# y halves, odd-head order, a three-pass first slab, and five attention-stage weight remainders on GpSimd

## The chip, the cores and the metric

The kernel runs on one core of one Trainium2 chip. TensorE multiplies matrices, VectorE, ScalarE and GpSimd do elementwise work, and SyncE and GpSimd issue DMAs. The time is that of the device, in microseconds, for one execution of the whole program on 256 tokens of width 1024; lower is better. Engine times below come from one profiled execution.

## What is computed

Two blocks run one after the other. The first has a retention layer and a sparse-attention layer, each with a mixture of experts. The second has three branches on one input projection:

```python
def second_block(x, w_in, ...):
    u = h @ w_in
    z, xbc, dt_f_raw, dt_b_raw, q, k, v, gate_logits = jnp.split(u, ...)
    y_ssd = ssd_branch(z, xbc, dt_f_raw, dt_b_raw, ...) @ w_proj_ssd
    y_att = attention_branch(q, k, v) @ w_proj_attn
    mix = (gates[:, :, 0] * y_ssd + gates[:, :, 1] * y_att) @ w_out
    h = layer_norm_2(alpha * h + mix, ln1_g, ln1_b)
    f = jnp.square(jax.nn.relu(h @ w_up)) @ w_down
    return layer_norm_2(alpha * h + f, ln2_g, ln2_b)
```

`ssd_branch` starts with a centred depthwise convolution of five taps over the 24 x 128 channels of `xbc`, then scans in both directions, multiplies by silu(z) and normalizes by group. `attention_branch` has 12 heads with windows of three dilations.

## The kernel before

Every engine has its own program, written out by hand; the engines meet at semaphores (`wait_ge` on one, `then_inc` on the other). The program goes through the stages in the list `STAGES`.

**Weight slabs.** Dense weights come in slabs of 128 x 4096 floats through three slots of `ring`, loaded by SyncE (`dense`). A matrix product is made from three products of rounded parts: `high(q)` on ScalarE (L1639) rounds a half slab into `w_rounded`, `low(q)` on VectorE (L2105) writes the remainder, `ring` minus `w_rounded`, into `ring_low`, and TensorE (`split_columns`, L854) multiplies rounded by rounded, rounded by remainder and remainder by rounded, interleaved. A half slab is 48 matmuls of 256 columns. The counters `w_high` and `w_low` count halves in order; `q` numbers the halves over the whole program, and `HQ["att"]` is the first half of the attention stage. `w_rounded` has two buffers, so `high(q)` waits until TensorE is done with half q - 2.

**Start.** SyncE loads the transposed tokens and the two halves of the first slab, then the next two slabs. GpSimd waits for the first slab and then issues the retention constants (`cret`), the constants of all stages (`call`), the tokens (`h`) and the first gain and bias, in this order, and folds the router's weights. VectorE makes the activations' remainder, `low(0)`, `low(1)`, and then waits for `cret` before `low(2)`. TensorE starts with `pe.wait_ge(x_low, 1)` and `split_slabs("ret_in", 8, r_hT)`, whose first half waits for `low(0)`.

**Attention stage.** Its 12 halves of weights (`xbc_half(n)`, six slabs) feed the convolution; they are laid between the steps of the 12 heads. For a head `hd` TensorE does `att_transposes` (L970), for even heads also `att_scores` of the next pair (L1404), then `att_products` (L1425) and `xbc_half(hd + 2)`. ScalarE copies the transposes out of PSUM (L1933), runs `high(HQ["att"] + hd + 3)`, copies a finished slab to `c_raw` (L1941), makes the exponentials for head `hd + 2` (L1922) and the silu after the convolution (L1914). VectorE does, for each head, `att_largest(hd + 2)` (L2706, L2710, L2711: mask, row maximum, its scaling), `att_out(hd)` (L2716: products out of PSUM), `low(HQ["att"] + hd + 3)`, and `conv(hd)` (L2692 the first tap of two channels, L2694 the other four). Four PSUM banks go round for transposes, scores and products; `take_aux(b)` waits until bank b - 4 is read, so an even head's products wait for `att_out` of the odd head before. GpSimd copies `s_a3` at the start of the stage (L790) and has nothing else until the scan.

**Scan stage (ssd).** Sixteen steps p, four to a group g. VectorE makes clamped decays (`clamp`, L2823), `weigh_decay` (L2812), `take_y` (L2833: y out of PSUM, half a group at a time), `root_diagonal` (L2858) and remainders; ScalarE the exponentials (L1982); GpSimd the scaled inputs (L808). TensorE's `diagonals(p)` (L1528) write y of group g into one pair of PSUM banks, the same pair for every group. A group's first `diagonals` waits in `take_pair` until the whole pair has been read for the group before.

**Work on GpSimd that is read below.** `plain_features` (L766) adds two 128 x 2048 tensors; `fold_norm` has small products (L745, L749).

Of the kernel before, what the change touches and what calls it, by code (L numbers as in the profile page):

```python
# [22 lines left out]
F32 = mybir.dt.float32  # L23
# [129 lines left out]
def build(nc, x_tok, x_feat, slabs, experts_w, c_all, c_ret, c_nsa, c_ssd, c_att, w_pattn, ln_gb, out):  # L153
    ctx = ExitStack()
    with ctx:
# [286 lines left out]
        decay_ready = sem("decay_ready")  # L442
        rows_ready, ssd_exp_ready = sem("rows_ready"), sem("ssd_exp_ready")
        ssd_y_ready, square_ready = sem("ssd_y_ready"), sem("square_ready")
        root_ready, root_diag_ready, y_low = sem("root_ready"), sem("root_diag_ready"), sem("y_low")
        mix_ready, f_ready = sem("mix_ready"), sem("f_ready")
        x_high, x_low, x_plain = sem("x_high"), sem("x_low"), sem("x_plain")
# [274 lines left out]
        def _(pool):  # L722

            pool.wait_ge(slab_loaded[0], 16)
            pool.dma_start(cret, c_ret).then_inc(stage_loaded, 16)
            pool.dma_start(call[:], c_all).then_inc(call_loaded, 16)
            pool.dma_start(h[:], x_tok).then_inc(h_loaded, 16)

# [60 lines left out]
            for u in range(3):  # L789
                nc.gpsimd.tensor_copy(s_a3.rearrange("p (r i u h) -> p r i u h", r=2, i=NT, u=3)[:, :, :, u, :],  # L790
                                      s_a.rearrange("p i (r h) -> p r i h", r=2)).then_inc(copies_ready, 1)
            nc.gpsimd.memset(s_half, -0.5).then_inc(pool_chain, 1)

            def root(g):
# [26 lines left out]
        def _(pe):  # L821
# [68 lines left out]
            def first_slab(stage, src, ln, signal, count):  # L890

                dst = take_pair(PJ[stage])
                for half in range(2):
# [23 lines left out]
                                                            stop=(half == 1 and n == 2 and k == 3))  # L917
                    last.then_inc((half_done, slab_done)[half], 1)

            def split_slabs(stage, n, src, first=0):  # L920
                for s in range(first, n):
                    dst = take_pair(PJ[stage] + s)
                    for q in (HQ[stage] + 2 * s, HQ[stage] + 2 * s + 1):
                        (split_columns if by_columns(q) else split_rows)(dst, q, src)
# [70 lines left out]


            SPLIT = ((0, 0), (0, 1), (1, 0))
            pe.wait_ge(x_low, 1)
            split_slabs("ret_in", 8, r_hT)

            def ret_transposes(hd):

# [432 lines left out]
            for hd in range(ATT_H - 2):  # L1435
                att_transposes(hd)
                if hd % 2 == 0:
                    att_scores(hd // 2 + 1)
                att_products(hd)
                xbc_half(hd + 2)  # L1440
            for hd in (ATT_H - 2, ATT_H - 1):
                att_transposes(hd)
            for hd in (ATT_H - 2, ATT_H - 1):
# [75 lines left out]
            def diagonals(p):  # L1519

                g, c = divmod(p, 4)
                j = PJ["ssd"] + 2 * g
                dst = (take_pair(j) if c == 0 else pair(j))[:, c * T:(c + 1) * T]
                pe.wait_ge(xdt_ready, p + 1)
                pe.wait_ge(m_ready, 2 * p + 2)
                for n, (r, i, a, b, at) in enumerate(((0, 0, 0, T, 0), (0, 1, P, T, 256), (1, 0, 0, P, 384), (1, 1, 0, T, 512))):
                    for e in range(2):
                        last = nc.tensor.matmul(dst[e * DH:(e + 1) * DH, a:b], s_xdt[:, p % 4, r, i, e * DH:(e + 1) * DH],  # L1528
                                                s_M[:, (2 * p + e) % 4, at:at + b - a], start=(n == 0), stop=(n == 3))
                last.then_inc(diag_done, 1)  # L1530
# [559 lines left out]
        def _(dve):  # L2090
# [630 lines left out]
            low(HQ["att"] + 2)  # L2721
            for hd in range(ATT_H - 2):
                att_largest(hd + 2)
                att_out(hd)
                low(HQ["att"] + hd + 3)
                conv(hd)
            att_out(ATT_H - 2)
            att_out(ATT_H - 1)
            for hd in (ATT_H - 2, ATT_H - 1):
# [97 lines left out]
            def take_y(g, half):  # L2827
# [7 lines left out]
                if half:  # L2835
                    last.then_inc(pair_out[j % 2], 1)
                    wait_pair_out(dve, j)
                else:
                    link(last)

            def gate_y(g):

# [300 lines left out]
```

## Time and profile before

| what | us |
|---|---|
| median of 3 runs (1504.03 to 1506.44) | 1504.74 |
| the profiled execution | 1504.41 |
| its span, first to last instruction | 1502.6 |
| TensorE busy (matmul), share of the span | 1425.3, 95% |
| VectorE busy | 800.4, 53% |
| ScalarE busy | 551.8, 37% |
| GpSimd busy | 58.0, 4% |

The shares are means over stages with different limits: in the expert stages the DMA queues are full, in the dense stages TensorE is. The attention stage lies between about 955 and 1053 us of the span, the scan stage between about 1095 and 1207. Busy times of an engine count overlapping instructions once.

### The profile page before, as it was taken

The page shows a single profiled execution, that of the slowest core. Times are in us where ns is not written, and L with a number is a line of the kernel's source. Part 1 is how long each engine was busy: PE and PEld are TensorE (multiplying, and loading weights), DVE is VectorE, ACT ScalarE, POOL GpSimd, SP SyncE. Part 2 cuts the span into 40 slices and gives each one's busy share as a digit, 9 for nine tenths or more (in the row PEclk, how much of TensorE's full clock was granted, in tenths as well). Part 3 has the DMA queues.
Part 4 walks back from the last instruction along what each step waited for, and adds up shares of the span by engine and source line. Part 5 has one row for each costly group of instructions (what it writes and reads, how often), then busy time and mean ns, then how long its engine had stood idle before and what let it go on. Part 6 is the DMA issues. An engine that isn't in the chain of part 4 may idle for free. (4 is left out here: it accounts for less than half of the span.)

```text
span 1502.6 us, 20186 instructions
## 1 busy us (share of the span) xinstructions
PE 1425.3 (95%) x8684; PEld 1064.0 (71%) x8684; DVE 800.4 (53%) x1105; ACT 551.8 (37%) x701; POOL 58.0 (4%) x79
## 2 busy tenths in 40 slices
PE   6999999999988999999999979999988899999997
PEld 6987785443437788874434349899967799799886
DVE  4645552221227657551222254699899955655545
ACT  3344442111013354421101024588656553344432
POOL 1000000000003000000000010100111100000000
PEclk9999999999999999999999999999998999999999
DMA  8553686999994540389999974533411144445451
GB/s 342 176 215 114 252 334 265 429 427 427 429 426 165 175 162 1 113 314 416 427 427 428 428 331 165 210 113 123 159 57 57 57 168 169 177 154 202 170 194 58
DMA packets 27745, 355.16 MB, mean 236 GB/s; under 512 B 2881, under 2 KB 4929, under 8 KB 5761
## 3 DMA queue, kind: packets, MB, share of 16 engines
q1 hardware_dynamic: 25840, 341.85, 57.4%
q0 software_dynamic: 1808, 11.93, 2.1%
q8 instruction: 72, 1.18, 0.3%
q14 instruction: 25, 0.20, 0.0%
HBM read 352.72 MB, written 1.05 MB: 235 GB/s over the span
## 5 line engine op out<-in xcount | busy, mean ns | idle before, releaser
L2105 DVE TENSOR_TENSOR ring_low<-ring,w_rounded 128x2048 fp32r<-128x2048 f32 (+1 forms) x124 | 290.5, 2347 | 244.2 <-ACT w_rounded L1639 236.1
L1639 ACT ACTIVATE w_rounded<-ring 128x2048 fp32r<-128x2048 f32 (+1 forms) x124 | 235.2, 1899 | 311.7 <-PE ps L854 97.4
L854 PE MATMUL ps<-split,w_rounded 128*128 128x256 f32 x960 | 228.9, 286 | 17.5 <-DVE ring_low L2105 16.5
L854 PE MATMUL ps<-split,ring_low 128*128 128x256 f32 x736 | 209.7, 285 | 0.0
L854 PEld LDWEIGHTS ps<-split,w_rounded 128*128 128x128 f32 x960 | 168.7, 193 | 18.7 <-issue 16.2
L854 PE MATMUL ps<-hT_low,w_rounded 128*128 128x256 f32 x512 | 145.3, 284 | 0.0
L854 PEld LDWEIGHTS ps<-split,ring_low 128*128 128x128 f32 x736 | 141.2, 192 | 0.0
L884 PE MATMUL ps<-w_rounded,split 128*128 128x512 f32 (+1 forms) x352 | 124.5, 394 | 2.9 <-DVE split L2926 1.5
L2398 DVE TENSOR_SCALAR split<-ps,work 128x1024 fp32r<-128x1024 f32 x14 | 18.0, 1284 | 198.2 <-PE ps L1154 198.2
L1122 PE MATMUL ps<-work 128*64 128x512 f32 x448 | 100.9, 597 | 4.5 <-DMA work<-experts_w 4.5
L884 PE MATMUL ps<-ring_low,split 128*128 128x512 f32 (+1 forms) x256 | 99.0, 387 | 0.0
L854 PEld LDWEIGHTS ps<-hT_low,w_rounded 128*128 128x128 f32 x512 | 98.9, 193 | 0.0
L1122 PE MATMUL ps<-ring,work 128*64 128x512 f32 x416 | 93.9, 596 | 0.0
L960 PE MATMUL ps<-w_rounded,split 128*128 128x512 f32 x320 | 87.1, 392 | 0.0
L884 PEld LDWEIGHTS ps<-w_rounded,split 128*128 128x128 f32 x352 | 66.8, 190 | 17.8 <-DVE split L2926 1.9
L1122 PEld LDWEIGHTS ps<-work 128*64 128x64 f32 x448 | 30.8, 137 | 63.6 <-issue 59.5
L1729 ACT ACTIVATE work<-ps 128x512 f32<-128x512 f32 x32 | 17.4, 594 | 149.2 <-PE ps L1102 149.2
L1154 PE MATMUL ps<-work 128*64 128x512 f32 x320 | 70.8, 593 | 0.1
L960 PEld LDWEIGHTS ps<-w_rounded,split 128*128 128x128 f32 x320 | 59.9, 188 | 13.5 <-issue 0.8
L1122 PEld LDWEIGHTS ps<-ring,work 128*64 128x64 f32 x416 | 28.3, 137 | 52.9 <-issue 52.9
L2393 DVE TENSOR_TENSOR work<-work,ps 128x512 f32<-128x512 f32 x16 | 11.0, 688 | 98.4 <-PE ps L1122 98.4
L884 PE MATMUL ps<-w_rounded,hT_low 128*128 128x512 f32 (+1 forms) x160 | 60.7, 380 | 0.0
(368 smaller groups left out, 2438.3 us busy)
## 6 DMA issues: line engine op xcount, KB each, us to landing
ring<-slabs SPq DMA_DIRECT2D x65, 2048.0 KB, 8.1
work<-experts_w SPq DMA_DIRECT2D x48, 2048.0 KB, 20.7
ring<-experts_w SPq DMA_DIRECT2D x36, 2048.0 KB, 16.9
w_plain<-experts_w SPq DMA_DIRECT2D x12, 2048.0 KB, 16.7
gb<-ln_gb POOLq DMA_DIRECT2D x6, 1024.0 KB, 8.8
ring<-slabs SPq DMA_DIRECT2D x2, 1024.0 KB, 8.7
hT<-x_feat SPq DMA_DIRECT2D x1, 1024.0 KB, 5.0
work<-c_ret POOLq DMA_DIRECT2D x1, 1024.0 KB, 11.9
```

The costliest lines, as they stand in the source:

```text
L854: last = nc.tensor.matmul(dst[:, at:at + T], w3[a][:, k, c * P:(c + 1) * P], src[b][:, k, :], start=(k == 0 and t == 0), stop=(k == KC - 1 ...
L884: last = nc.tensor.matmul(dst[:, i * 512:i * 512 + cols], src[a][:, 4 * half + k, i * P:(i + 1) * P], w3[b][:, k, :], start=(half == k == ...
L960: last = nc.tensor.matmul(dst[i][:, c * 512:(c + 1) * 512], src(a, s)[:, 2 * half + k, i * P:(i + 1) * P], w3[b][:, k, c * 512:(c + 1) * 512],
L1122: last = nc.tensor.matmul(bank(b)[e * CAP:(e + 1) * CAP, :], m_xT[:, e2 % 3, 4 * half + k, e * CAP:(e + 1) * CAP], w4[:, e, k, :], start=( ...
L1154: last = nc.tensor.matmul(bank(4 + c)[e * CAP:(e + 1) * CAP, :], m_heT[:, 2 * half + k, e * CAP:(e + 1) * CAP], w4[:, e, k, c * 512:(c + 1 ...
L1639: nc.scalar.activation(rounded_half(q), half_of(ring, q), ACT.Copy).then_inc(w_high, 1)
L1729: last = nc.scalar.activation(m_xT[:, (2 * t + e) % 3, 4 * half:4 * half + 4, :], tok[:, :, e, :], ACT.Copy)
L2105: V.tensor_tensor(half_of(ring_low, q), half_of(ring, q), rounded_half(q).bitcast(F32), ALU.subtract).then_inc(w_low, 1)
L2393: V.tensor_tensor(m_he, m_sg, bank(1), ALU.mult).then_inc(ps_.he_ready, 1)
L2398: V.tensor_scalar(m_yh, bank(4, 2), m_w[:, e2:e2 + 1], None, ALU.mult).then_inc(ps_.weighed, 1)
```

## The change

Five things change, all in the hand-written orders.

- GpSimd waits for the third slab before it issues `c_all`, the tokens and what follows.
- TensorE's first half slab is done by a new function in three passes (rounded by rounded, rounded weights by remainder of the activations, remainder of the weights), each with its own wait.
- In the attention stage TensorE does `xbc_half(hd + 2)` before `att_products(hd)` for odd heads; VectorE does `att_out(hd)` after `conv(hd)` for odd heads.
- The remainders `low(HQ["att"] + hd + 3)` of even heads 0, 2, 4, 6 and 8 are made by GpSimd; VectorE's next remainder waits for them.
- The first two `diagonals` of a group wait for the first half of `take_y` of the group before, and the third waits for the second half.

```diff
@@ block.gpsimd
             pool.dma_start(cret, c_ret).then_inc(stage_loaded, 16)
+            pool.wait_ge(slab_loaded[2], 16)
             pool.dma_start(call[:], c_all).then_inc(call_loaded, 16)
             pool.dma_start(h[:], x_tok).then_inc(h_loaded, 16)
...
+            for hd in range(0, ATT_H - 2, 2):
+                q = HQ["att"] + hd + 3
+                pool.wait_ge(w_high, q + 1)
+                pool.wait_ge(w_low, q)
+                nc.gpsimd.tensor_tensor(half_of(ring_low, q), half_of(ring, q), rounded_half(q).bitcast(F32),
+                                        ALU.subtract).then_inc(w_low, 1)
             nc.gpsimd.memset(s_half, -0.5).then_inc(pool_chain, 1)
@@ block.tensor
+            def start_half(dst):
+
+                pe.wait_ge(x_high, 1)
+                pe.wait_ge(w_high, 1)
+                w3 = split_weights(0, KC)
+                for n in range(3):
+                    if n == 1:
+                        pe.wait_ge(x_low, 1)
+                    elif n == 2:
+                        pe.wait_ge(w_low, 1)
+                    for c in range(2):
+                        for k in range(KC):
+                            last = nc.tensor.matmul(dst[:, c * T:(c + 1) * T], w3[n // 2][:, k, c * P:(c + 1) * P],
+                                                    r_hT[n % 2][:, k, :], start=(n == c == k == 0),
+                                                    stop=(n == 2 and c == 1 and k == KC - 1))
+                last.then_inc(half_done, 1)
...
-            pe.wait_ge(x_low, 1)
-            split_slabs("ret_in", 8, r_hT)
+            first_pair = take_pair(PJ["ret_in"])
+            start_half(first_pair)
+            split_columns(first_pair, 1, r_hT)
+            split_slabs("ret_in", 8, r_hT, 1)
...
-                att_products(hd)
-                xbc_half(hd + 2)
+                if hd % 2:
+                    xbc_half(hd + 2)
+                    att_products(hd)
+                else:
+                    att_products(hd)
+                    xbc_half(hd + 2)
...
-                dst = (take_pair(j) if c == 0 else pair(j))[:, c * T:(c + 1) * T]
+                dst = (take_pair(j) if p == 0 else pair(j))[:, c * T:(c + 1) * T]
+                if c == 0 and g:
+                    pe.wait_ge(y_half_out, g)
+                if c == 2 and g:
+                    wait_pair_out(pe, j - 2)
@@ block.vector
                 att_largest(hd + 2)
-                att_out(hd)
-                low(HQ["att"] + hd + 3)
+                if hd % 2 == 0:
+                    att_out(hd)
+                if hd % 2:
+                    dve.wait_ge(w_low, HQ["att"] + hd + 3)
+                    low(HQ["att"] + hd + 3)
                 conv(hd)
+                if hd % 2:
+                    att_out(hd)
...
-                    link(last)
+                    last.then_inc(y_half_out, 1)
+                    dve.wait_ge(y_half_out, g + 1)
```

## Rows read from the trace of the kernel before

**Rows 1.** Busy time by engine: stretch, length, busy (instructions), granted clock, DMA.

```profile
967.00:1049.10 82.10, 78.20 (x643) 74.44 (x642) 77.87 (x147) 69.39 (x100) 0.00 (x0) 1.00 0.36 129
1095.00:1207.00 112.00, 95.49 (x754) 81.16 (x754) 105.84 (x206) 63.05 (x68) 16.14 (x27) 0.91 0.18 64
```

**Rows 2.** TensorE's waits, 966 to 1049: us in total, times, longest.

```profile
PE ps L1425 <- ACT work L1933: 3.9, 5, 0.8
```

**Rows 3.** TensorE's longest wait in the scan, 1095 to 1207.

```profile
PE ps L1528 <- DVE work L2833: 10.3, 3, 4.8
```

**Rows 4.** VectorE's waits, 1095 to 1210.

```profile
DVE ring_low L2105 <- ACT w_rounded L1639: 3.4, 4, 0.9
DVE work L2833 <- PE ps L1528: 1.7, 1, 1.7
```

**Rows 5.** In order of time, an odd head to the next: start, length, instruction.

```profile
991.75 0.60 PE L970 MATMUL ps<-call,work 128*128 128x128 f32 x4
992.88 1.90 ACT L1639 ACTIVATE w_rounded<-ring 128x2048 fp32r<-128x2048 f32 x1
994.93 2.28 DVE L2105 TENSOR_TENSOR ring_low<-ring,w_rounded 128x2048 fp32r<-128x2048 f32 x1
997.13 0.61 DVE L2692 TENSOR_SCALAR work<-work 128x256 f32<-128x256 f32 x2
997.77 3.63 DVE L2694 SCALAR_TENSOR_TENSOR work<-work 128x256 f32<-128x256 f32 x8
...
1000.97 1.90 ACT L1639 ACTIVATE w_rounded<-ring 128x2048 fp32r<-128x2048 f32 x1
1001.43 1.10 PE L1425 MATMUL ps<-work 128*128 128x64 f32 x8
1002.34 0.36 PE L854 MATMUL ps<-split,w_rounded 128*128 128x256 f32 x1
...
1008.18 0.60 PE L970 MATMUL ps<-call,work 128*128 128x128 f32 x4
```

**Rows 6.** VectorE by line, two heads (983.3 to 999.8): busy, mean ns of one.

```profile
L2710 DVE TENSOR_REDUCE work<-work 128x2 f32<-128x512 f32 x2 | 1.4, 686 | 0.1
L2706 DVE SCALAR_TENSOR_TENSOR work<-work,ps 128x512 f32<-128x512 f32 x2 | 1.4, 684 | 0.1
L2716 DVE COPY work<-ps 128x128 f32<-128x128 f32 x2 | 0.6, 285 | 0.0
```

**Rows 7.** In order of time: GpSimd beside VectorE's remainders, and GpSimd's fold.

```profile
24.78 1.73 POOL L745 TENSOR_TENSOR folded<-call 128x128 f32<-128x128 f32 x1 [10.50 <-DMA call<-c_all]
27.62 0.40 POOL L749 TENSOR_TENSOR folded<-call 128x128 f32<-128x128 f32 x1
...
465.18 2.28 DVE L2105 TENSOR_TENSOR ring_low<-ring,w_rounded 128x2048 fp32r<-128x2048 f32 x1
465.44 6.51 POOL L766 TENSOR_TENSOR hT<-split,split 128x2048 f32<-128x2048 f32 x1 [2.90 <-DVE split L2113]
467.38 6.72 DVE L2105 TENSOR_TENSOR ring_low<-ring,w_rounded 128x2048 fp32r<-128x2048 f32 x1
```

**Rows 8.** In order of time: scalings by a column, beside GpSimd and without.

```profile
1137.93 3.48 POOL L808 TENSOR_TENSOR work<-work 128x256 f32<-128x256 f32 x6
1140.51 0.98 DVE L2858 TENSOR_SCALAR work<-call,work 128x128 f32<-128x128 f32 x2
...
1202.26 0.48 DVE L2858 TENSOR_SCALAR work<-call,work 128x128 f32<-128x128 f32 x2
```

**Rows 9.** In order of time: the start of the program.

```profile
10.73 2.29 DVE L2105 TENSOR_TENSOR ring_low<-ring,w_rounded 128x2048 fp32r<-128x2048 f32 x1 [0.70 <-ACT w_rounded L1639]
13.17 0.55 PE L854 MATMUL ps<-split,w_rounded 128*128 128x256 f32 x1 [13.17 <-DVE ring_low L2105]
23.95 2.29 DVE L2105 TENSOR_TENSOR ring_low<-ring,w_rounded 128x2048 fp32r<-128x2048 f32 x1 [7.95 <-DMA work<-c_ret]
27.42 0.28 PE L854 MATMUL ps<-split,w_rounded 128*128 128x256 f32 x1
```

More of the change, by code:

```diff
@@ L444, in build @@
         ssd_y_ready, square_ready = sem("ssd_y_ready"), sem("square_ready")
+        y_half_out = sem("y_half_out")
         root_ready, root_diag_ready, y_low = sem("root_ready"), sem("root_diag_ready"), sem("y_low")
```

## The prediction, made before the change was run

> **What bounds the kernel now.** I read the three places that the change touches, each by the same views in the same order: the busy time of the engines in the stretch, then who waits there and for whom, then the instructions in order of time. In the attention stage (heads 0 to 9) TensorE is busy 78.20 of 82.10 us and VectorE 77.87 [rows 1]: two engines are full at once, and a microsecond taken from one is worth only what the other lets through. TensorE's only waits there are five of 0.78, for ScalarE's copy of an odd head's transposes [rows 2]; they come to 3.9 us. In the scan stage of the second block (1095 to 1207) VectorE is busy 105.84 of 112.00 us and TensorE 95.49 [rows 1]. The reader sees TensorE wait 10.3 us in three waits for the VectorE line that takes y out of PSUM [rows 3], while VectorE itself waits for ScalarE four times 0.85 and for TensorE once, 1.7, at the end [rows 4]. VectorE sets that stage. At the start, TensorE begins at 13.17, after the first weight remainder, and later has its second slab at 27.42 [rows 9].
>
> **Three-pass first slab and the held-back loads: about -1.0 us.** The first half needs only the rounded weights to begin. Its remainder starts on VectorE at 10.73, which is when rounding is done; the old first matmul came 0.15 after the remainder's end at 13.02 [rows 9], so the new one comes at about 10.85, 2.3 earlier. Of its 48 matmuls the first 16 want no remainder and the next 16 only that of the activations, which VectorE has just finished; a slab's 96 now take 27.42 - 13.17, 0.15 each, so the 33rd comes 4.7 after the first, past 13.02. The second slab doesn't profit as much: its remainder stands on VectorE behind the wait for the retention constants and starts at 23.95 [rows 9]. That load is issued as before, ahead of the new wait, so I leave its landing where it is. The remainder ends at 26.24, TensorE goes on at 26.39, against 27.42: 1.03 gained, and a wait of 1.3 opens in front of it. The bounds are 0 and 2.3 (were the constants to land early enough). The constants for later and the token tile move behind the third slab on GpSimd's queue, with the first gain and bias load and the router's fold queued behind them; the first reader on TensorE is the second retention head's transposes, nine slabs on, which is what hides them: cost nothing; without that cover they would cost what they land later.
>
> **The y halves: 0.** The wait of the first two diagonals of a group moves from the second half's copy to the first half's, made two steps earlier; the 10.3 us of TensorE waits [rows 3] go. But the next thing on the path is VectorE's own queue, which runs on without a pause through these three places: all its waits in the stage are the four on ScalarE, whose rounding is behind exponentials that wait for VectorE, and the 1.7 us at the last diagonals [rows 4], which the change leaves alone. TensorE comes early to the next wait for VectorE. Bounds: a gain of up to 3.4, if the ScalarE waits all went, and a loss of 0.3; I take 0, the row of the saturated engine being the nearer.
>
> **The odd-head order alone: no gain.** TensorE now does the odd head's half slab before its products, so the 0.78 is covered. In return VectorE copies the odd products out after the convolution, and the next even head's products wait for that bank. Follow the rows from an odd head's transposes [rows 5]: transposes at 991.75, rounding ends at 994.78, remainder starts at 994.93 (3.18 in all), convolution follows 2.20 later and takes 4.27 (997.13 to 1001.40), the copy 0.28 [rows 6], the even products 0.91 (1001.43 to 1002.34), the half slab 5.84 (to 1008.18), and there the next odd transposes stand: 16.68 us around. The pair of heads takes 16.43 now (991.75 to 1008.18). So with the remainders left on VectorE or moved at no cost, the pair stays at 16.4 to 16.7; the 3.9 of rows 2 turn into waits for a PSUM bank.
>
> **Five remainders on GpSimd: about +11 us.** Off VectorE go five times 2.20 (one remainder, start to next start [rows 5]). On GpSimd the nearest row is an addition of the same size, 128x2048 with two inputs in SBUF: 6.51 [rows 7]. It is shorter than it looks. It began at 465.44, while VectorE's remainder ran until 467.46; the next remainder, which takes 2.28 everywhere else, took 6.72 and ended at 474.10, which is 2.15 after GpSimd's end at 471.95 [rows 7]. The two took turns: GpSimd's own part is 471.95 - 467.46, 4.49. A small GpSimd multiplication shows the same: 1.73 begun under a remainder, 0.40 alone [rows 7]. So a remainder on GpSimd holds off whatever on VectorE can't run beside it for 4.49.
>
> What can't? Remainders, by these rows. The convolution's first tap is a scaling of one SBUF tensor by a column; the nearest row is the two scalings of the identity, 0.98 for two beside a running GpSimd, 0.48 with GpSimd idle [rows 8]: held too. The other eight instructions of a convolution take two SBUF inputs, as the remainders do, but none ran beside GpSimd in this trace. The Trainium skill (SBUF — State Buffer, section "Who interferes with whom") has it that an instruction of VectorE with two SBUF inputs contends with a GpSimd instruction that reads SBUF, and that whoever is first keeps the pair for its whole length. By that rule all ten are held and the sum is the one below; by the rows alone the eight are open, which is the first rival. The stage's free work is what reads PSUM or reduces: 0.69 + 0.69 a head [rows 6].
>
> The sum for a pair: 16.43 - 2.20 + 4.49 = 18.72 if the whole hold falls on held work, 17.3 if one head's 1.38 lies under it. That is +0.9 to +2.3 a pair. Where the hold falls into the loop of the odd head (its convolution, then the copy, then the even products), the pair takes 16.68 + 4.49 = 21.2, +4.7. GpSimd gets its rounded half at about 1002.87 in the time of this trace and TensorE wants the remainder at 1008.8, 0.6 after the transposes at 1008.18 [rows 5]: 4.49 and up to 0.48 for the instruction in progress fit, so TensorE doesn't wait for GpSimd but for VectorE. Of five transfers I take the first at nothing (VectorE has just been waiting for the slabs there and has room), one at 4.7, three at 2.3, and with the order's small gain for the first pair, -0.5, that is 11.1; say +11. Bounds: 5 x 0.9 = 4.5 with nothing in the loop, and 4.7 + 4 x 2.3 = 13.9. VectorE's wait for the previous remainder, new on odd heads, has its own remainder, the convolution and the copy queued behind it, and the even products wait for that copy; it is over before the rounding that the same remainder needs, so it costs nothing. After the heads VectorE's own list (combination weights, gates) sets when TensorE goes on, so the delay is passed on.
>
> **Sum.** The profiled execution is 1504.41 (span 1502.6), within 0.4 of the median 1504.74. 1504.4 - 1.0 + 0 + 0 + 11 = 1514.4.
>
> **The rivals.** First, on the other side: the eight two-input instructions of the convolution are not held. Then GpSimd's 4.49 lies beside them, the pair stays at the odd loop's 16.4 to 16.7, and the whole is 1504.4 - 1.0 + 0.2 = 1503.6: not slower. It decides where the convolution's row beside a running GpSimd stays at 0.48 an instruction. For it speaks that no row here shows that case; against it, that the remainders and the scalings are both held. Chance 0.12. Second: TensorE's waits do come back, 10.3 in the scan and 3.9 at the heads, on top of free transfers: 1504.4 - 1.0 - 14.2 = 1489; it needs VectorE to have slack that rows 1 and 4 don't show; half of it, 1497, is as far as I can imagine. Chance 0.06. Third: GpSimd's subtraction needs 6.5 of its own. Then a pair takes 16.43 - 2.20 + 6.5 = 20.7, five of them +21.5, the whole 1525; against it, the turns in rows 7. Chance 0.04. That the moved remainders don't run beside anything (GpSimd busy with older work) can be left out: its queue is empty between the copies at the start of the stage and the scan.
>
> **How the numbers follow.** The forecast, held convolutions, has 0.78: 1514.4, from 1506.6 (4.5, and 2.3 at the start) to 1518.3 (13.9 and a start gain of 0). The range 1506.0 to 1519.0 holds that case and leaves out the first rival and most of the others. What a measurement of this kernel can tell from no change is about 0.2%, 3 us. Slower by more: 0.74 of the forecast and 0.04 of the third rival, 0.78. Within: the rest of the forecast and most of the first rival, 0.15. Faster: the second and a part of the first, 0.07.
>
> **What would show it.** Right: GpSimd rows of 4.5 to 4.9 in the attention stage; in each pair a scaling or a tap of the convolution (or the small scaling of the row maxima) stretched by 3 to 4.5; TensorE's 0.78 gone and waits on VectorE's copy of odd products in their place, 1 to 7 us each; the scan stage as long as now with its 10.3 moved to other VectorE lines; the second slab near 26.4. Wrong: taps that stay at 0.48 beside GpSimd, a pair of heads at 15.7 (the order paid), or a scan stage under 110 us.

## The result, and the profile after

The changed kernel takes 1515.99 us (median of 4 runs, 1515.22 to 1522.02) against 1505.59 of the kernel before beside it: 10.4 more, a ratio of 1.0070 (95% interval 1.0053 to 1.0088). The profiled execution took 1516.13, its span is 1514.3, 11.7 more than before. Line numbers move with the change: L854 became L862, L970 L995, L1425 L1452, L1528 L1563, L2105 L2140, L2692 and L2694 L2727 and L2729, L2706 to L2711 L2741 to L2746, L2716 L2751, L2833 L2873.

The span splits at two marks, the transposes of head 0 and those of head 10, read from the timelines:

| stretch | before | after | difference |
|---|---|---|---|
| to the transposes of head 0 | 966.99 | 969.29 | +2.30 |
| heads 0 to 9 | 82.11 | 91.54 | +9.43 |
| from there to the end | 453.50 | 453.47 | -0.03 |

Busy times of the stretches after, as in [rows 1]: the five pairs of heads, all ten heads, and a piece of the scan stage as long as the one before.

```profile
969.29:984.65 15.36, 15.36 (x131) 14.82 (x129) 13.38 (x18) 8.47 (x14) 4.61 (x1) 1.00 0.38 138
984.65:1009.57 24.92, 17.41 (x131) 16.79 (x130) 20.05 (x35) 15.73 (x23) 4.65 (x1) 0.86 0.23 85
1009.57:1026.15 16.58, 15.41 (x131) 14.80 (x130) 16.19 (x28) 13.96 (x21) 4.59 (x1) 1.00 0.36 127
1026.15:1043.59 17.44, 15.41 (x130) 14.79 (x130) 17.02 (x30) 14.82 (x22) 4.59 (x1) 1.00 0.34 121
1043.59:1060.83 17.24, 15.42 (x131) 14.80 (x130) 16.82 (x30) 14.57 (x22) 4.64 (x2) 1.00 0.33 123
969.29:1060.83 91.54, 79.00 (x643) 76.00 (x641) 83.46 (x137) 67.55 (x98) 23.07 (x6) 0.96 0.32 116
1107.26:1219.26 112.00, 96.61 (x758) 82.03 (x759) 106.12 (x207) 64.16 (x68) 18.45 (x27) 0.92 0.20 69
```

One pair of heads, the second, holds most of the loss: 24.92 us against 16.43, at a mean granted clock of 0.86. The first pair is shorter than before, the other three are 0.15 to 1.0 longer. In the scan VectorE is as busy as before.

The waits, for [rows 2 to 4]: TensorE's in the heads; TensorE's in the scan; VectorE's in the scan.

```profile
PE ps L1452 <- DVE work L2751: 12.5, 4, 7.5
...
PE ps L1573 <- ACT y L2024: 7.6, 3, 3.5
PE ps L1563 <- DVE work L2852: 4.1, 5, 1.3
...
DVE ring_low L2140 <- ACT w_rounded L1674: 3.1, 4, 0.8
DVE work L2873 <- PE ps L1563: 1.7, 1, 1.7
```

TensorE no longer waits for ScalarE's copies but for the copy of the odd products, 12.5 us in four waits, one of them 7.5. In the scan the 10.3 for y is gone; 7.6 stand in its place at the sums of squares (`square_sums`, L1573), which the same stage makes from ScalarE's squares. All of TensorE's waits there come to 16.7 before and 16.5 after, and VectorE's two waits are those of before.

The second pair in order of time, and a later hold, for [rows 5 to 7] (a row of several instructions has the time from the first to the last):

```profile
985.71 7.87 DVE L2729 SCALAR_TENSOR_TENSOR work<-work 128x256 f32<-128x256 f32 x8
988.46 5.12 DVE L2729 SCALAR_TENSOR_TENSOR work<-work 128x256 f32<-128x256 f32 x2
988.65 4.65 POOL L798 TENSOR_TENSOR ring_low<-ring,w_rounded 128x2048 fp32r<-128x2048 f32 x1 [11.63 <-ACT w_rounded L1674]
993.50 0.28 DVE L2751 COPY work<-ps 128x128 f32<-128x128 f32 x1
993.83 1.97 PE L1452 MATMUL ps<-work 128*128 128x64 f32 x8 [7.51 <-DVE work L2751]
996.56 0.41 PE L862 MATMUL ps<-hT_low,w_rounded 128*128 128x256 f32 x1
998.60 0.28 PE L862 MATMUL ps<-split,w_rounded 128*128 128x256 f32 x1
...
1012.68 4.59 POOL L798 TENSOR_TENSOR ring_low<-ring,w_rounded 128x2048 fp32r<-128x2048 f32 x1 [19.39 <-ACT w_rounded L1674]
1012.99 0.69 DVE L2745 TENSOR_REDUCE work<-work 128x2 f32<-128x512 f32 x1
1013.71 3.59 DVE L2746 TENSOR_SCALAR work<-work 128x2 f32<-128x2 f32 x1
...
1029.85 1.10 PE L1452 MATMUL ps<-work 128*128 128x64 f32 x8 [2.03 <-DVE work L2751]
```

The second row is the end of the first: the tap that was running when GpSimd began was done in its usual 0.48, and the next one waited until GpSimd had finished. The eight taps took 7.87 instead of 3.63; the copy and the even products stood behind them. In the third pair the maximum ran beside GpSimd in its usual 0.69, and the scaling after it, of two columns, took 3.59 where 0.17 is usual. From that scaling VectorE runs without a wait to the copy of head 5's products, for which the even products of the fourth pair wait 2.03: the third remainder is paid in the fourth pair.

While TensorE stood still, the clock that the chip granted it fell to half, and it stayed there after the wait. The windows of 3 us around the wait that ended at 993.83, the same columns as above (the granted clock is the third number from the right):

```profile
991.00:994.00 3.00, 0.17 (x1) 0.17 (x1) 3.00 (x3) 0.00 (x0) 2.30 (x1) 0.56 0.03 11
994.00:997.00 3.00, 3.00 (x15) 3.00 (x16) 2.35 (x7) 1.65 (x5) 0.00 (x0) 0.50 0.02 5
997.00:1000.00 3.00, 3.00 (x22) 3.00 (x22) 2.89 (x8) 1.63 (x3) 0.00 (x0) 0.80 0.00 0
```

0.50 is the lower of the two levels, 1.2 GHz: a matmul takes 0.41 at 996.56 and 0.28 at 998.60, when it was back at 2.4.

The start, for [rows 9]:

```profile
10.83 3.75 PE L940 MATMUL ps<-split,w_rounded 128*128 128x256 f32 x16 [10.83 <-ACT w_rounded L1674]
...
24.06 2.29 DVE L2140 TENSOR_TENSOR ring_low<-ring,w_rounded 128x2048 fp32r<-128x2048 f32 x1 [8.07 <-DMA work<-c_ret]
...
26.41 0.39 PE L862 MATMUL ps<-split,w_rounded 128*128 128x256 f32 x1 [1.94 <-DVE ring_low L2140]
```

TensorE starts 2.3 earlier and stands at the second slab for 1.94. The load of the fifth slab, which SyncE issues when the second slab is done, is at 38.21 against 39.14.

### The profile page after: what moved, and what is told of

Same layout as the page of the kernel before. It is cut to its first block and busy times, and to the rows that moved or that the text cites. A ratio compares the mean times of both kernels' runs of the same rounds, so it can differ in the third digit from the quotient of the medians.

```text
span 1514.3 us, 20196 instructions
## 1 busy us (share of the span) xinstructions
PE 1429.3 (94%) x8684; PEld 1068.0 (71%) x8684; DVE 807.2 (53%) x1100; ACT 551.1 (36%) x701; POOL 84.1 (6%) x84
## 5 line engine op out<-in xcount | busy, mean ns | idle before, releaser
L2140 DVE TENSOR_TENSOR ring_low<-ring,w_rounded 128x2048 fp32r<-128x2048 f32 (+1 forms) x119 | 278.9, 2347 | 247.1 <-ACT w_rounded L1674 238.9
L862 PE MATMUL ps<-split,w_rounded 128*128 128x256 f32 x944 | 224.2, 286 | 4.2 <-DVE ring_low L2140 3.2
L862 PE MATMUL ps<-split,ring_low 128*128 128x256 f32 x720 | 204.8, 284 | 0.0
L862 PEld LDWEIGHTS ps<-split,w_rounded 128*128 128x128 f32 x944 | 165.4, 192 | 5.5 <-DVE ring_low L2140 2.4
L862 PE MATMUL ps<-hT_low,w_rounded 128*128 128x256 f32 x496 | 140.5, 283 | 0.0
L862 PEld LDWEIGHTS ps<-split,ring_low 128*128 128x128 f32 x720 | 137.9, 192 | 0.0
L862 PEld LDWEIGHTS ps<-hT_low,w_rounded 128*128 128x128 f32 x496 | 95.5, 193 | 0.0
```

The lines of the kernel that those rows point to most:

```text
L862: last = nc.tensor.matmul(dst[:, at:at + T], w3[a][:, k, c * P:(c + 1) * P], src[b][:, k, :], start=(k == 0 and t == 0), stop=(k == KC - 1 ...
L2140: V.tensor_tensor(half_of(ring_low, q), half_of(ring, q), rounded_half(q).bitcast(F32), ALU.subtract).then_inc(w_low, 1)
```

## The experiments

In all of them the time is set beside runs of the kernel before on the same chip. The heads and the pairs are those of the profiled execution, and these are the sharper measure: the heads begin anywhere from 965.26 to 973.63 in these executions, mostly for differences in the two expert stages, which nothing here touches.

| run | median us | ratio (95%) | heads | pairs |
|---|---|---|---|---|
| before | | | 82.11 | 16.42, 16.43, 16.43, 16.42, 16.42 |
| change | 1515.99 | 1.0070 (1.0053 to 1.0088) | 91.54 | 15.35, 24.92, 16.58, 17.45, 17.23 |
| e1 | 1505.09 | 0.9992 (0.9979 to 1.0005) | 81.50 | 15.35, 16.54, 16.56, 16.51, 16.53 |
| e2 | 1523.61 | 1.0107 (1.0090 to 1.0124) | 97.15 | 16.39, 22.46, 19.92, 19.91, 18.47 |
| e3 | 1512.27 | 1.0042 (1.0019 to 1.0065) | 86.86 | 15.32, 20.26, 16.61, 17.42, 17.25 |
| e4 | 1522.75 | 1.0107 (1.0090 to 1.0124) | 97.85 | 15.89, 24.63, 16.54, 24.21, 16.57 |
| e5 | 1508.02 | 1.0014 (0.9998 to 1.0031) | 83.90 | 15.35, 18.21, 16.54, 17.25, 16.54 |
| e6 | 1513.10 | 1.0039 (1.0023 to 1.0056) | 89.25 | 15.35, 20.20, 16.59, 20.49, 16.61 |
| e7 | 1506.66 | 0.9997 (0.9984 to 1.0009) | 84.03 | 15.35, 19.08, 16.53, 16.53, 16.53 |
| e8 | 1504.77 | 0.9989 (0.9973 to 1.0005) | 81.99 | 15.36, 17.03, 16.54, 16.53, 16.53 |
| e9 | 1503.17 | 0.9975 (0.9963 to 0.9987) | 79.68 | 15.36, 15.66, 16.21, 16.24, 16.21 |
| e10 | 1501.74 | 0.9978 (0.9965 to 0.9992) | 78.85 | 15.36, 16.19, 15.71, 15.85, 15.73 |
| e11 | 1505.06 | 0.9995 (0.9980 to 1.0010) | 82.13 | 16.42, 16.43, 16.43, 16.43, 16.43 |
| e12 | 1515.07 | 1.0072 (1.0045 to 1.0098) | 91.59 | 15.36, 24.94, 16.61, 17.43, 17.25 |

### All remainders on VectorE (e1)

```diff
-            for hd in range(0, ATT_H - 2, 2):
...
-                if hd % 2:
-                    dve.wait_ge(w_low, HQ["att"] + hd + 3)
-                    low(HQ["att"] + hd + 3)
+                low(HQ["att"] + hd + 3)
```

> The change with its five remainders back on VectorE; the start, the odd-head order and the y halves stay. Theory (GpSimd's instruction keeps VectorE's instructions on SBUF waiting, and that alone is the loss): no pair of heads is longer than 16.7 us (16.43 before), TensorE's longest wait in the attention stage is under 2 us, and the whole is 1503.5 to 1505.5 against 1505.6 of before and 1516.0 of the change. Rival (the order of the odd heads costs, with the even products behind the copy): the pair of heads is over 17 and the whole 1510 or more.

The window of its second pair, and TensorE's waits in the heads (L2745 is here the copy of the products):

```profile
982.43:998.97 16.54, 15.41 (x131) 14.80 (x130) 15.89 (x31) 14.21 (x20) 0.00 (x0) 1.00 0.36 129
...
PE ps L1446 <- DVE work L2745: 4.5, 4, 1.1
```

The theory held: with the start, the odd order and the y halves alone the kernel is at the level of before. The loss is GpSimd's five instructions: 91.54 - 81.50, 10.0 us in the heads. What the fifth of them costs comes behind the heads: from head 10 to the transposes ahead of the scan (1105.17 in the change) the change takes 44.34, e1 43.83 and the kernel before 43.82. The odd order trades ScalarE's 0.78 for 1.1 at the bank, as the loop worked out in the prediction said, and gains 1.07 in the first pair alone.

### The five remainders alone (e2)

```diff
+            for hd in range(0, ATT_H - 2, 2):
+                q = HQ["att"] + hd + 3
...
                 att_out(hd)
-                low(HQ["att"] + hd + 3)
+                if hd % 2:
+                    dve.wait_ge(w_low, HQ["att"] + hd + 3)
+                    low(HQ["att"] + hd + 3)
                 conv(hd)
```

> The kernel before with only the five remainders moved to GpSimd, in the old order of the heads, so that VectorE copies the odd products out ahead of the convolution. Theory: each remainder takes 4.5 to 4.9 and stretches a convolution or a scaling of VectorE by 3 to 4.5, but no even product waits for a held convolution; a pair then costs 0.9 to 2.3 more, no single wait of TensorE is near 7.5, and the whole is 1509 to 1516. Rival (the loss needs the new order): under 1507.

Waits in its heads: TensorE's, and ScalarE's for the scaling of the row maxima (L2717) and for the transposes:

```profile
PE ps L1431 <- ACT work L1939: 13.9, 5, 4.7
...
ACT work L1928 <- DVE work L2717: 18.2, 6, 4.5
ACT work L1939 <- PE ps L976: 11.5, 4, 3.2
```

The expectation was too low: 15.0 us more in the heads than before, not five times 0.9 to 2.3, and a median above the range. I had looked at VectorE alone. Four of the five remainders hold the scaling of the row maxima for 4.6, ScalarE's exponentials wait for that scaling, and the copy of the odd head's transposes stands behind them on ScalarE. In the old order TensorE's odd products come next and wait 2.8 to 4.7 for the copy; in the new order a half slab lies in between. So the odd order, which gains next to nothing by itself, makes the moved remainders cheaper, 10.0 instead of 15.0. Much of that difference is clock: the wait of 4.74 and the first two of 2.8 went with a stretch at half the clock each, and what the pairs lost beyond their waits is 5.1 in e2 against 2.0 in the change.

### Head 2's remainder back on VectorE (e3)

```diff
-            for hd in range(0, ATT_H - 2, 2):
+            for hd in (0, 4, 6, 8):
...
+                if hd == 2:
+                    low(HQ["att"] + hd + 3)
                 if hd % 2:
```

> The change with the remainder of head 2 alone back on VectorE (four stay on GpSimd). Theory: in the change the pair of heads 2 and 3 took 24.92 us, because the remainder began under the convolution of head 1 and the even products, 7.51 late, waited behind it; the other pairs took 15.4 to 17.4. Without it the wait of 7.51 goes, and with it TensorE's stretch at half clock: 7 to 9 us less, 1507 to 1509. Rival (every remainder costs about 2, wherever it falls): 1514. A third outcome would be that another remainder now begins under a convolution and brings the wait back in another pair: 1514 to 1517 with a wait of 5 or more at a later even head.

Its first pair's scaling, held by the first remainder, and the second pair, where no GpSimd instruction runs:

```profile
973.38 4.60 DVE L2746 TENSOR_SCALAR work<-work 128x2 f32<-128x2 f32 x1
...
986.64 3.63 DVE L2729 SCALAR_TENSOR_TENSOR work<-work 128x256 f32<-128x256 f32 x8
990.53 0.66 PE L1452 MATMUL ps<-work 128*128 128x64 f32 x4 [3.30 <-DVE work L2751]
```

4.7 us of the heads came back, not 7 to 9, and the median, 1512.27, is above the expected 1507 to 1509. The wait of 7.51 didn't go, it became 3.30, and these are the first remainder's: VectorE, 4.4 late from the first pair on, pays in the second. So of the 7.51, 1.13 are the loop's own (e1), 2.17 come from the first remainder, and 4.21 from the second, whose hold on the tap was 4.72 - 0.48 = 4.24. The first is the hold less the remainder that VectorE no longer makes, 4.60 - 0.17 - 2.20 = 2.23; the second has its full price, because VectorE's relief comes behind the even products that wait. The pair also ran for a while at half the clock: 20.26 - 16.54 - 2.17 leaves 1.55 for that.

### The hold without anything to wait for (e4) and without reading (e5)

Both are e1, in which VectorE makes all remainders, with an addition on GpSimd: the first loop body of the diff in e4, the second in e5.

```diff
+            for hd in range(0, ATT_H - 2, 2):
...
+                nc.gpsimd.tensor_tensor(scratch, scratch, scratch, ALU.subtract).then_inc(scratch_done, 1)
...
+                for n in range(3):
+                    nc.gpsimd.memset(scratch[:, 0:1720], 0.0).then_inc(scratch_done, 1)
```

> As the first of these runs (VectorE makes all remainders), but GpSimd makes, at the same points, a subtraction of the same size on a buffer that nobody reads (the gains and biases, loaded after the heads instead of before). Nobody waits for GpSimd. Theory (the hold, not the lateness of the remainder, is what costs): GpSimd's rows are 4.5 to 7, a remainder, tap or scaling of VectorE is stretched by 2 to 4.6 beside each, and the whole is 1512 to 1525, although no engine needs what GpSimd makes. Rival (the remainder that comes later from GpSimd is the cost): as the first run, 1503.5 to 1505.5.

> As the run with the subtraction on a buffer that nobody reads, but GpSimd fills that buffer with zeros instead: three fills of 128x1720 behind one another, 4.5 us in all, which write SBUF and read nothing. Theory (it is GpSimd's reading of SBUF beside an instruction of VectorE with two SBUF inputs that holds): taps and remainders stay at 0.48 and 2.29 beside the fills; at most the scalings of one input are stretched, by up to 1.5 each; the whole is 1504 to 1508. Rival (any work of GpSimd on SBUF holds VectorE off): stretches of 1.5 and more on taps too, and 1512 or more.

In e4, GpSimd, the tap that it meets, and TensorE's waits:

```profile
988.35 4.22 DVE L2731 SCALAR_TENSOR_TENSOR work<-work 128x256 f32<-128x256 f32 x2
988.55 3.74 POOL L799 TENSOR_TENSOR gb<-gb 128x2048 f32<-128x2048 f32 x1 [13.84 <-ACT w_rounded L1676]
...
PE ps L1454 <- DVE work L2753: 16.2, 4, 7.3
```

In e5, three fills beside a scaling of the row maxima, a remainder and the first taps, and three more beside the last taps of another convolution:

```profile
971.66 4.76 POOL L800 MEMSET gb<- 128x1720 f32 x3 [11.78 <-ACT w_rounded L1677]
971.71 1.52 DVE L2749 TENSOR_SCALAR work<-work 128x2 f32<-128x2 f32 x1
971.99 2.28 DVE L2143 TENSOR_TENSOR ring_low<-ring,w_rounded 128x2048 fp32r<-128x2048 f32 x1
974.18 2.38 DVE L2730 TENSOR_SCALAR work<-work 128x256 f32<-128x256 f32 x2
...
986.75 1.40 DVE L2732 SCALAR_TENSOR_TENSOR work<-work 128x256 f32<-128x256 f32 x3
987.45 4.72 POOL L800 MEMSET gb<- 128x1720 f32 x3 [11.02 <-ACT w_rounded L1677]
```

e4 settles that the hold is the cost: nobody reads what GpSimd makes, and the heads take 16.35 more than in e1 (about 4.2 of it at half the clock after the waits of 7.27 and 6.62). Its subtractions are shorter, 3.60 to 3.74 (inputs and output are one buffer), yet it loses more than the change, since VectorE makes its remainders as well and two of the five meet taps. e5 settles what is held by what. Beside fills, which only write, remainders stay at 2.28 and taps of two SBUF inputs at 0.48, but the one-input scalings wait for the end of the fill: that of the row maxima takes 1.52 instead of 0.17, the two first taps 2.38 instead of 0.61. The heads lose 2.4 instead of 16.35; the median, 1508.02, is at the upper end of what was expected. The Trainium skill (SBUF — State Buffer, section "Who interferes with whom") says the same of these cases: an instruction with two SBUF inputs contends with a GpSimd instruction that reads SBUF and not with one that only writes it, a scaling can contend with GpSimd, and a reduction never does. The rows agree: the tap took 4.72 beside a remainder and 0.48 beside a fill, the scaling 4.60 and 1.52, the maximum 0.69 beside a remainder.

### Where the hold falls (e6), and how long it is (e7, e8)

```diff
                 pool.wait_ge(w_low, q)
+                pool.wait_ge(conv_ready, hd)
...
+                nc.gpsimd.tensor_tensor(half_of(ring_low, q)[:, 0:4], half_of(ring, q)[:, 0:4],
+                                        rounded_half(q).bitcast(F32)[:, 0:4], ALU.subtract).then_inc(part_low, 1)
```

e6 is the change with the wait alone. In e7 and e8 GpSimd also begins after the convolution and makes a part of each remainder, `0:4` of eight chunks in e7 and `0:2` in e8; VectorE makes the rest.

> The change, with GpSimd's remainders held back until VectorE has done the odd head's convolution, so that none begins under a tap. Theory (where the hold falls decides): the second remainder now begins at the copy of head 1's products instead of under its taps; about 1.7 of its 4.6 lie beside the copy, the masked sum and the maximum, which are not held; the pair of heads 2 and 3 falls from 24.92 to 19 to 21, TensorE's longest wait from 7.5 to 3.3 or less, the whole from 1516.0 to 1509 to 1512. Rival (the lateness of the remainder itself counts): the wait stays or moves to the remainder's reader on TensorE, 1515 or more.

> The change with half of each of the five remainders on GpSimd (1024 of 2048 columns), begun after the odd head's convolution, and the other half on VectorE. Theory: GpSimd's rows are 2.2 to 2.4; 1.4 to 1.7 of each lie beside unheld work, so a scaling is stretched by 0.6 to 1.0 while VectorE saves 1.1: pairs of 16.0 to 16.5, and the whole 1503 to 1506, at the level of the run with all remainders on VectorE (1505.1). Rival (each use of GpSimd costs by being there, not by its length): 1510 or more.

> The same with a quarter of each remainder on GpSimd (512 columns). Theory: rows of 1.1 to 1.3, wholly beside the copy, the masked sum and the maximum, so that no instruction of VectorE is stretched; VectorE saves 0.57 a pair, the pairs come to 15.9 to 16.2, and the whole to 1502 to 1504, the fastest of these. Rival (VectorE isn't what sets the pair): 1505 to 1506.

The scaling that e6's second remainder holds in place of a tap, a window of its fourth pair, and TensorE's waits in e6; then e8's third pair, and VectorE's waits there:

```profile
989.62 3.20 DVE L2747 TENSOR_SCALAR work<-work 128x2 f32<-128x2 f32 x1
...
1024.00:1027.00 3.00, 3.00 (x15) 3.00 (x16) 2.93 (x3) 2.06 (x2) 3.00 (x1) 0.50 0.75 317
...
PE ps L1453 <- DVE work L2752: 7.7, 4, 3.3
```

```profile
1000.43:1016.97 16.54, 15.41 (x130) 14.80 (x130) 15.52 (x31) 14.85 (x22) 1.28 (x1) 1.00 0.35 128
...
DVE ring_low L2141 <- ACT w_rounded L1675: 2.6, 4, 0.8
```

e6 came out as its theory put it for the second pair: 20.20, the longest wait 3.27. But the fourth pair took 20.49, at half the clock after a wait of 2.03 which in the change was followed by none; so of the 4.7 that the second pair gained, 2.3 are left in the heads, and the median, 1513.1, is above the range.

e7 and e8 are the dose. The first remainder's hold on the scaling is 4.60, 2.40 and 1.29 for whole, half and quarter, and the wait that it leaves in the second pair is 3.30, 2.20 and 1.62 (1.13 without GpSimd): about half of the hold each time. The other half is what VectorE is relieved of, 2.20, 1.07 and 0.54 from start to next start: the hold beyond the usual 0.17, less this relief, is 2.23, 1.16 and 0.58, and the waits grew by 2.17, 1.07 and 0.49. In e7 the wait of 2.20 was followed by half the clock, so its second pair took 19.08, far above the expected 16.0 to 16.5. The medians, 1506.66 and 1504.77, are a little above both ranges, and e8's stands nearer to its rival's. But my theory of the other pairs fell. They take 16.53 in e1, e7 and e8 alike, within 0.03. In e7 VectorE's relief of 1.1 is used up by the scaling that its half holds, 1.44 instead of 0.17. In e8 the scaling takes 0.32, so that 0.4 of the 0.54 are left; VectorE spends them waiting for ScalarE's rounding (0.60 to 0.76 a pair, 0.22 in e1), and the pair is as long as ever. What sets it is the odd head's loop, not VectorE's sum of work.

### The remainder out of the loop (e9, e10)

The edit of e9, against e1:

```diff
                 if hd % 2 == 0:
                     att_out(hd)
-                low(HQ["att"] + hd + 3)
+                    low(HQ["att"] + hd + 3)
                 conv(hd)
                 if hd % 2:
                     att_out(hd)
+                    low(HQ["att"] + hd + 3)
```

In e10 the even head's remainder is split as in e8, and GpSimd begins its quarter when VectorE has made the odd head's remainder.

> The change with all remainders on VectorE, as in the first of these runs, and the odd head's remainder moved behind its convolution and the copy of its products. There each pair took 16.53 us whatever VectorE was relieved of. Theory (the odd head's loop, rounding, remainder, convolution, copy, even products, sets the pair): with the remainder of 2.29 out of the loop the next bound is VectorE's own work, 15.6 a pair, or TensorE's, 15.35: pairs of 15.4 to 16.0, the heads 77 to 80 instead of 81.5, the whole 1500.5 to 1503.5. Rival (TensorE then waits for that remainder instead, at the next even head's weights): pairs of 16.4 to 17.5 and 1504 to 1509.

> The same, with a quarter of each even head's remainder (512 columns) on GpSimd, begun when VectorE's remainder of the odd head is done, so that its 1.28 lie beside the masked sum and the maximum. Theory: out of the loop, relief of VectorE now counts: the pairs come to TensorE's own 15.35 to 15.6, the heads to 77 to 78, the whole to 1499 to 1502. Rival (TensorE waits for the late remainder): as the run before, 1504 to 1509.

The third pair of e9, TensorE's waits in its heads, and VectorE's masked sums with the only wait of VectorE there (3.0, in the first pair); then all heads of e10:

```profile
1001.96:1018.17 16.21, 15.53 (x130) 14.88 (x130) 15.79 (x31) 14.85 (x22) 0.00 (x0) 1.00 0.36 129
...
PE ps L856 <- DVE ring_low L2134: 2.0, 3, 0.7
...
L2735 DVE SCALAR_TENSOR_TENSOR work<-work,ps 128x512 f32<-128x512 f32 x10 | 6.8, 680 | 3.0 <-PE ps L1425 3.0
```

```profile
967.05:1045.89 78.84, 77.55 (x642) 74.40 (x641) 75.04 (x148) 68.88 (x99) 6.49 (x6) 1.00 0.37 134
```

e9 is faster than the kernel before beyond its interval, 0.9975, with pairs of 15.66 to 16.24 (expected 15.4 to 16.0): the loop was the bound, and the rival's wait for the late remainder is there too, 0.7 in each of three pairs. Once the loop is broken, VectorE's own list is the next bound. Its instructions of a pair take 16.2 from start to start, 16.17 of the 16.21 in e9's third pair. My 15.6 was the busy time of [rows 1] shared out over five pairs; it left out the small steps between instructions, and the first pair has a wait of 3.0 in it. In e10 the same quarter that bought nothing in e8 takes 0.4 to 0.5 from each of the last three pairs, and 0.8 from the heads; its pairs, 15.7 to 16.2, and its heads are above what I expected, its median within the range, and between e9 and e10 as a whole no difference is measured (0.9975 and 0.9978). Both beat the change, and the kernel before by a quarter of a per cent.

### The rest by itself, and the change again (e11, e12)

e11 is the kernel before with the parts of the diff that concern the start and the y halves, and no other. e12 is the change, unaltered.

> The kernel before with the three-pass start, the held-back loads and the y halves alone; heads as before. Theory: TensorE begins near 10.8 and is 0.9 to 1.0 earlier than before at its second slab; the heads take 82.1; TensorE's waits for y of 10.3 us move to other instructions and the scan takes the same 112 within 0.7; the whole is 0 to 1 below before, 1505 to 1506. Rival (the waits for y come back as time): 1495 to 1500.

> The change once more, for a second profile. Theory (holds at the same places, since the engines' order is fixed): the second remainder begins under the taps of head 1 again, the pair of heads 2 and 3 takes 23 to 25.5, and the heads 90 to 93. Rival (where the hold falls is chance of an execution): another pair is the long one, or none.

e11, TensorE's first wait in the scan and the scan's window:

```profile
PE ps L1563 <- ACT y L2014: 7.6, 3, 3.5
...
1095.00:1207.00 112.00, 97.79 (x757) 83.33 (x758) 105.74 (x207) 62.75 (x68) 18.43 (x27) 0.91 0.18 63
```

e12, TensorE at its second slab, and two windows, the second pair of heads and the stretch after that second slab's wait:

```profile
26.57 0.39 PE L862 MATMUL ps<-split,w_rounded 128*128 128x256 f32 x1 [2.50 <-DVE ring_low L2140]
...
983.50:1008.44 24.94, 17.45 (x131) 16.83 (x130) 20.04 (x35) 15.71 (x23) 4.65 (x1) 0.86 0.24 85
...
26.00:31.00 5.00, 4.43 (x25) 4.43 (x26) 5.00 (x6) 0.07 (x1) 0.08 (x1) 0.67 0.91 382
```

In e11 the waits for y went and came back as waits for ScalarE's squares (L1563 is here `square_sums`). From the start of VectorE's first copy of y to that of its last the scan took 94.2, against 94.4 before. e12 repeats the change to 0.1 us in every pair. The holds fall where the order of the engines puts them; they aren't chance.

## Why the prediction was right, and where it was lucky

The forecast was 1514.4, 10.0 above the time before; measured are 10.4 between the medians (8.0 to 13.2 by the interval of the ratio), and 8.4 in e12. The parts that the profile shows, 9.4 in the heads, 0.9 of gain at the start and nothing behind the heads, come to 8.5, so how near the total lies to the forecast is partly chance. The mechanism, GpSimd's instruction holds VectorE's instructions on SBUF off, was the right one, and e4 shows it apart from everything else. By its steps:

- **Start, -1.0.** The second slab was put at 26.39 and came at 26.41; the fifth slab's load is 0.93 earlier. What I missed is that the new wait in front of the second slab can bring the clock down. In four of the twelve executions with the new start (e4, e5, e8, e12) that wait, 2.2 to 2.7 long, was followed by a stretch at half the clock, and the fifth slab's load was 0.7 to 1.1 later than before, not earlier (e3, with 2.3, kept its clock). A loss belonged inside the bounds.
- **y halves, 0.** Right: the 10.3 moved to the next wait, VectorE's chain in the scan stayed as it was to 0.2 (e11), and e11's ratio, 0.9995, is no gain beyond its interval.
- **Odd order, no gain.** Right: 16.68 was worked out for the loop, e1 has 16.51 to 16.56, and the first pair gains 1.07 (I had said 0.5).
- **Five remainders, +11.** GpSimd's own part, 4.49 by the turns of [rows 7], is 4.59 to 4.65. The heads grew by 9.43 with the order in it, where I summed 11.1. The terms are off one by one (each is paid where its hold reaches TensorE: the first two in the second pair, the third in the fourth, the fourth in the fifth, the fifth behind the heads):

| remainder | predicted | measured against e1 |
|---|---|---|
| first | 0 | 2.17, paid in the second pair (e3) |
| one in the loop | 4.7 | 4.21 |
| half clock after the wait of 7.51 | not in the sum | 2.0 (24.92 - 16.54 - 7.51 + 1.13) |
| the other three | 2.3 each | 0.94, 0.70, and about 0.5 behind the heads |
| third pair, which has none to pay | | 0.02 |
| all in the heads | 11.6 | 10.04 |

The first remainder wasn't free: VectorE had indeed waited before it, but that room was used up before the hold began. The other three were overpriced by about 4.8, because I took the upper end of 0.9 to 2.3. Their holds began under the masked sum, the maximum ran beside them too, and the scaling behind it lost 3.42, 3.22 and 3.28; less the 2.20 that VectorE no longer spends, and less the 0.22 that it had waited a pair in e1, the first two leave 1.0 and 0.8, and 0.94 and 0.70 were paid. That is the lower end, a hold with one head's unheld work beside it. What the third leaves is less than this, and part of the stretch behind the heads is at half the clock (0.96 on average); it wasn't taken apart. The clock made up for part of the overpricing. So the total was right with errors of opposite sign in it, and that was luck.

- **The bound in the heads.** I read VectorE, 77.87 busy of 82.10, as one of two full engines, and priced time on it as time of the pair. For time added that was right to about 0.2 a pair, as the third and fourth remainder show. Time taken off is another matter: e8 shows that 0.4 us less a pair buys nothing in the new order, and e9 that 2.29 moved out of the odd loop, with VectorE's work unchanged, buy 0.3 a pair (0.9 in the second), until VectorE's own 16.2 bind. The loop was in my own working (16.68, measured 16.53), but I used it only to judge the order.
- **The rivals.** The taps were held (4.72 beside GpSimd), so the first falls; no wait of TensorE came back as time (e11), so the second falls; the subtraction needs 4.6, not 6.5, so the third falls. The signs named for the right case appeared: GpSimd rows of 4.6, a tap or scaling stretched by 3.2 to 4.4 in each pair, waits of 1.2 to 7.5 for the copy of the odd products.

The 11.7 of the profiled spans have 2.3 from ahead of the heads, where the start should have given 0.9 back. In e12 the same kernel's heads begin 1.15 earlier, in e11, with the same start, at 966.94. Of the 3.2 lost between, 1.9 lie in the first expert stage and 1.3 in the sparse-attention layer behind it, and they vary between executions of one kernel; what sets them wasn't tried.

## What to carry over

Before an elementwise instruction is moved from VectorE to GpSimd, list what VectorE does in the time that it will take: whatever reads two SBUF operands, or scales one, waits for GpSimd's end, and even a two-column instruction can wait 4.6 us; in these runs only instructions with an operand in PSUM, and reductions, ran beside GpSimd's reading unheld. The price is the hold less what VectorE is relieved of, and without the relief where the hold falls into the loop. Then look for the loop that sets the period: relief of a busy engine buys nothing outside it, and putting 2.3 us of VectorE's work at another place in its own order gave more than moving it to another engine. A hold that seems to vanish into slack may be paid one round later, and a wait of TensorE can cost again by the clock that follows.

## What the runs showed of the hardware that I had not expected

- A scaling of 128x2 waited for the whole of a GpSimd instruction, 4.60, while beside such an instruction a maximum over 128x512 took its usual 0.69 and the masked sum, one of whose inputs is in PSUM, its usual 0.68 (e6).
- Beside fills by GpSimd the same scaling waited (1.52), and the copy out of PSUM right behind it ended with it (1.45 instead of 0.28), but the remainder behind these in VectorE's program ran at its usual 2.28 from 971.99 on, beside the scaling that had not ended.
- Half-clock stretches went with all waits of TensorE from 3.27 to 7.51 in the heads, and with some shorter ones: twice 2.77 (e2), 2.20 (e7), 2.03 (e6) and, at the start, 2.17 to 2.69 in four executions. With others of that length the clock stayed: 2.81 (e5), 2.80 (e2), 2.32 at the start (e3), 2.03 and 1.82 (the change). What decides it in that range stays open.
- A subtraction on GpSimd of 128x2048 takes 4.6 from two buffers into a third, rounded, and 3.60 to 3.74 with one unrounded buffer as inputs and output; which of these shortens it wasn't tried.
